# Norm sums gathered on four rows in the token mixers, and the first convolution tap on ScalarE

## The reference

```python
def rmsnorm(x, g):
    y = x32 * lax.rsqrt(jnp.mean(x32 * x32, axis=-1, keepdims=True) + EPS)
def l2norm(x):
    return x32 * lax.rsqrt(jnp.sum(x32 * x32, axis=-1, keepdims=True) + EPS)

# token_mixers: GLA, RetNet, gated DeltaNet (GDN), Mamba-2 (SSD)
oa = rmsnorm(oa, gla_norm) * silu(gg)          # 4 heads of 128 channels; ret the same
cqkv = silu(causal_conv(dqkv, state, w))       # 4 taps, 1024 channels
q = l2norm(heads(cq, 4)) * GDN_DK ** -0.5      # 4 heads of 64 channels
k = l2norm(heads(ck, 4))
oc = rmsnorm(oc, gdn_norm) * silu(dg)
xbc = silu(causal_conv(sxbc, state, w) + b)    # 4 taps, 768 channels
od = rmsnorm(yd, ssd_norm)                     # 2 groups of 256 channels
out = sum(sigmoid(mg) * (branch @ w_branch)) @ w_out
```

## Time and profile before

| | |
|---|---|
| runs without profile | 2736.95, 2736.98 and 2749.7 us, median 2736.98 |
| profiled execution | 2750.4 us, of which the span of the trace is 2748.3 |
| busy, share of the span | PE 90%, DVE 59%, ACT 39%, POOL 7% |
| mean granted TensorE clock | 0.914 |
| reciprocals in the mixers | 10 on DVE: eight of 128x1152, two of 128x576 |
| first taps on DVE | 28, 12.4 us in all |

### The profile page before, as it was taken

One profiled execution on the slowest core, in us unless ns is written; L12 is line 12 of the kernel. 1 busy time (PEld: TensorE's weight loads), 2 busy tenths in 40 slices (PEclk: granted clock), 3 DMA queues, 4 the chain that ended last, 5 costly groups with the idle time before them and its releaser, 6 DMA issues.

```text
span 2748.3 us, 38217 instructions
## 1 busy us (share of the span) xinstructions
PE 2462.7 (90%) x14436; PEld 2124.5 (77%) x14436; DVE 1628.5 (59%) x2112; ACT 1074.4 (39%) x1450; POOL 178.8 (7%) x247
## 2 busy tenths in 40 slices
PE   8899868868999989889778879899999999999996
PEld 7788758857699978779678766678878778787786
DVE  4453554264366463544553443387887878778785
ACT  3322321112033343324221121166766667567563
POOL 0210101111000000211011201000000000000000
PEclk8889879778899999999889688799999999999999
DMA  5224321021345432323311122288988889889871
GB/s 192 93 82 141 117 74 50 31 97 39 137 146 166 164 129 93 105 103 115 125 54 47 59 70 72 90 309 301 333 294 317 303 300 331 294 299 321 299 282 74
DMA packets 122566, 456.43 MB, mean 166 GB/s; under 512 B 14056, under 2 KB 14474, under 8 KB 120018
## 3 DMA queue, kind: packets, MB, share of 16 engines
q1 hardware_dynamic: 118818, 432.66, 44.6%
q0 software_dynamic: 3632, 22.12, 2.2%
HBM read 443.72 MB, written 11.00 MB: 165 GB/s over the span
## 4 chain that ended last, share of the span: by engine, by line
PE 77%; DVE 11%; issue 5%; ACT 4%; DMA 1%; POOL 1%; DVEq 0%; SPq 0%; ACTq 0%; POOLq 0%
PE ps L715 9%; PE ps L717 8%; PE ps L716 8%; PE ps L762 5%; DVE weights_low L2220 4%; PE ps L1265 4%; PE ps L1267 3%; PE ps L1266 3%; PE ps L1287 3%; PE ps L1288 3%; PE ps L1289 3%; PE ps L1238 3%; PE ps L756 2%; PE ps L896 2%; DMA ring<-in_stream 1%
## 5 line engine op out<-in xcount | busy, mean ns | idle before, releaser
L715 PE MATMUL ps<-u_high,tiles_high 128*128 128x288 f32 x1688 | 535.1, 317 | 2.6 <-DVE arena L1712 2.6
L716 PE MATMUL ps<-u_low,tiles_high 128*128 128x288 f32 x1688 | 521.3, 309 | 0.0
L717 PE MATMUL ps<-u_high,tiles_low 128*128 128x288 f32 x1688 | 519.1, 307 | 0.0
L1688 DVE TENSOR_TENSOR tiles_low<-ring,tiles_high 128x1024 fp32r<-128x1024 f32 x238 | 291.7, 1229 | 268.7 <-ACT tiles_high L1346 267.6
L715 PEld LDWEIGHTS ps<-u_high,tiles_high 128*128 128x128 f32 x1688 | 340.8, 202 | 12.7 <-issue 6.7
L1346 ACT ACTIVATE tiles_high<-ring 128x1024 fp32r<-128x1024 f32 x238 | 250.7, 1054 | 245.9 <-DMA ring<-in_stream 155.9
L716 PEld LDWEIGHTS ps<-u_low,tiles_high 128*128 128x128 f32 x1688 | 341.0, 202 | 0.6
L717 PEld LDWEIGHTS ps<-u_high,tiles_low 128*128 128x128 f32 x1688 | 340.3, 202 | 0.0
L2220 DVE TENSOR_TENSOR weights_low<-expert_ring,weights_high 128x1024 fp32r<-128x1024 f32 x288 | 334.3, 1217 | 4.9 <-ACT weights_high L1597 2.2
L1265 PE MATMUL ps<-weights_high,u_high 128*128 128x512 f32 (+1 forms) x768 | 297.6, 388 | 23.2 <-DVE weights_low L2220 22.6
L2220 DVE TENSOR_TENSOR weights_low<-ring,weights_high 128x1024 fp32r<-128x1024 f32 x240 | 280.1, 1217 | 42.9 <-ACT weights_high L1597 41.8
(11 more groups left out here) (381 smaller groups left out, 3377.6 us busy)
## 6 DMA issues: line engine op xcount, KB each, us to landing
ring<-in_stream SPq DMA_DIRECT2D x530, 512.0 KB, 4.2
expert_ring<-in_stream SPq DMA_DIRECT2D x288, 512.0 KB, 5.5
arena<-in_state POOLq DMA_DIRECT2D x8, 1024.0 KB, 5.2
state_s<-arena POOLq DMA_DIRECT2D x8, 1024.0 KB, 4.2
const<-in_const SPq DMA_DIRECT2D x1, 2052.5 KB, 12.0
arena<-in_const POOLq DMA_DIRECT2D x2, 832.0 KB, 4.9
h<-in_x SPq DMA_DIRECT2D x1, 1152.0 KB, 5.1
y<-acc POOLq DMA_DIRECT2D x1, 1152.0 KB, 4.4
```

What stands on the lines that cost most here:

```text
L715: mm(out, hi[k], uh[:, k, :], start=k == 0, stop=False)
L716: mm(out, hi[k], ul[:, k, :], start=False, stop=False)
L717: last = mm(out, lo[k], uh[:, k, :], start=False, stop=k == KD - 1)
L1688: tt(t_low[:, q % HELD, :], ring[:, (t % RING) * TILE:(t % RING + 1) * TILE], t_high[:, q % HELD, :].bitcast(F32), ALU.subtract).then_inc( ...
```

## The change

- Output norm, all four mixers. `out_sums` uses a constant `row_of` (7 columns, a one in the fourth) so that block `r` lands in row `r` of one bank: four matmuls as before, but accumulated to 4x288 (for SSD rows 0 and 1). Root and reciprocal take 4x288.
- PE then spreads the rows back: `spread_rows`, one matmul of four contraction rows to a block, 128x288 out (4 matmuls, for SSD 2), into the banks in which the sums were. DVE multiplies out of PSUM.
- Because the spread values lie in the banks that `states` writes, `states` now waits for the reciprocal (`row_ready`), spreads, and then waits for `o_final`, that is, for DVE's product.
- Keys and queries. The sums go to 32 rows of one bank through `row_pick`, root and reciprocal take 32x288, and PE spreads with eight matmuls of 32 contraction rows onto 64 partitions each, after its fill slot 7. The reciprocal stands after block 6 of the convolution on DVE, not after block 7.
- Convolution. The first tap moves from DVE (L1908) to ACT, as an Identity with scale and bias, into three `cbuf` buffers in place of two, two blocks ahead; from the fourth block on it waits for the block three before to be finished.

```diff
 def out_sums(L, n):
-    pe.wait_ge(osq_ready, m + 1)
-        for b in range(4):
-            last = mm(bank(M + b)[:, 0:TOK], C("ones"), tmp4[:, b, :], start=True, stop=True)
+    pe.wait_ge(osq_ready, 5 * L + ROWS_AT[n] + 1)
+    for b in range(4):
+        r = b // 2 if n == SSD else b
+        last = mm(bank(M)[0:4, 0:TOK], C("row_of", 3 - r, 7 - r), tmp4[:, b, :], start=b == 0, stop=b == 3)
+def spread_rows(L, n):
+    pe.wait_ge(row_ready, 5 * L + ROWS_AT[n] + 1)
+    for b in range(2 if n == SSD else 4):
+        last = mm(bank(M + b)[:, 0:TOK], C("ident")[0:4, b:b + 1].to_broadcast([4, P]), rs4[0:4, 0, :],
+                  start=True, stop=True)
+    last.then_inc(row_ps, 1)
 def states(L, n):
-    pe.wait_ge(ort_ready, m + 1)
+    spread_rows(L, n)
     pe.wait_ge(o_taken, L * NHEAD + HBASE[n] + HEADS[n])
+    pe.wait_ge(o_final, m + 1)
...
 # ACT, conv()
+    tap(0)
+    tap(1)
     for b in range(NCONV[n]):
+        if b + 2 < NCONV[n]:
+            tap(b + 2)      # b + 2 >= 3: waits conv_ready
         fill(L, n, b)
         act.wait_ge(convsum_ready, c + 1)
...
 # DVE, out_norm()
-    V.reciprocal(rs4[:, 0:w, :], rs4[:, 0:w, :]).then_inc(dve_step, 1)
+    V.reciprocal(rs4[0:4, 0, :], rs4[0:4, 0, :]).then_inc(row_ready, 1)
+    dve.wait_ge(row_ps, 5 * L + ROWS_AT[n] + 1)
-        last = tt(o4, g4, rs4, ALU.mult)
+        last = tt(o4, g4, ps_t[:, M:M + 4, 0:TOK], ALU.mult)
```

More of the change, by code:

```diff
@@ L170, in constants @@
     c["slot_col"] = np.arange(P)[:, None] * 1.0
+    c["row_of"] = np.tile(np.arange(7)[None, :] == 3, (P, 1)) * 1.0
     c["ret_decay"] = c.pop("ret_decay")
@@ L230 @@
 Q_OF = {t: q for q, t in enumerate(SPLIT)}
+ROWS_AT = [0, 1, 3, 4]
+QK_ROWS = 2
 NORM_AT = {0: 0, 1: 1, 2: 2, 3: 3, 5: 4}
@@ L1012, in gdn @@
                 pe.wait_ge(state_new, 4 * L + 2)
-                pe.wait_ge(qksq_ready, L + 1)
+                pe.wait_ge(osq_ready, 5 * L + QK_ROWS + 1)
                 for b in range(4):
-                    last = mm(bank(M + b)[:, 0:TOK], C("halfones"), tmp4[:, b, :], start=True, stop=True)
-                last.then_inc(qksum_ps, 1)
+                    last = mm(bank(M)[0:32, 0:TOK], C("row_pick", 15 - b, 47 - b), tmp4[:, b, :], start=b == 0, stop=b == 3)
+                last.then_inc(osum_ps, 1)
                 for s in range(5, 8):
                     fill(L, GDN, s)
+                pe.wait_ge(row_ready, 5 * L + QK_ROWS + 1)
+                for b in range(4):
+                    for i in range(2):
+                        last = mm(bank(M + b)[64 * i:64 * i + 64, 0:TOK],
+                                  C("ident")[0:32, 16 * i + b:16 * i + b + 1].to_broadcast([32, 64]), rs4[0:32, 0, :],
+                                  start=True, stop=True)
+                last.then_inc(row_ps, 1)
                 fill(L, GDN, 8)
@@ L1456, in out_norm @@
                 fill(L, n, slot)
[L1457 to L1462, removed]
+                act.wait_ge(osum_ps, 5 * L + ROWS_AT[n] + 1)
+                A(rs4[0:4, 0, :], bank(M)[0:4, 0:TOK], ACT.Sqrt, scale=1.0 / (256 if n == SSD else 128),
+                  bias=C("eps")[0:4]).then_inc(ort_ready, 1)
                 for s in range(slot + 1, NSLOT[n]):
@@ L1477, in conv, with tap @@
             def conv(L, n):
+                def tap(b):
+                    ci = CONV0[n] + b
+                    if b == 0:
+                        act.wait_ge(pads_ready, 2 * L + (1 if n == GDN else 2))
+                        act.wait_ge(o_taken, L * NHEAD + HBASE[n])
+                    if b >= 3:
+                        act.wait_ge(conv_ready, 14 * L + ci - 2)
+                    A(cbuf[:, b % 3, 0:312], zblk(n, b)[:, 0:312], ACT.Identity, scale=PVc("conv_w", ci),
+                      bias=PVc("conv_b", ci)).then_inc(tap_ready, 1)
+                tap(0)
+                tap(1)
                 for b in range(NCONV[n]):
                     c = 14 * L + CONV0[n] + b
+                    if b + 2 < NCONV[n]:
+                        tap(b + 2)
                     fill(L, n, b)
@@ L1906, in conv @@
                     src = zblk(n, b)
-                    out = cbuf[:, b % 2, 0:312]
-                    ts(out, src[:, 0:312], wv[:, 0, ci:ci + 1], PVc("conv_b", ci), ALU.mult, ALU.add).then_inc(dve_step, 1)
-                    dve.wait_ge(dve_step, steps.next())
+                    out = cbuf[:, b % 3, 0:312]
+                    dve.wait_ge(tap_ready, 14 * L + ci + 1)
                     stt(out, src[:, 1:313], wv[:, 1, ci:ci + 1], out, ALU.mult, ALU.add).then_inc(dve_step, 1)
@@ L1917, in conv @@
                         fill(L, n, b - 1)
+                    if n == GDN and b == nb - 1:
+                        dve.wait_ge(ort_ready, 5 * L + QK_ROWS + 1)
+                        V.reciprocal(rs4[0:32, 0, :], rs4[0:32, 0, :]).then_inc(row_ready, 1)
                 finish(nb - 1)
@@ L2024, in gdn @@
                 conv(L, GDN)
[L2025 to L2029, removed]
+                dve.wait_ge(row_ps, 5 * L + QK_ROWS + 1)
+                stt(cv[:, 0:2, :], cv[:, 0:2, :], 0.125, ps_t[:, M:M + 2, 0:TOK], ALU.mult, ALU.mult)
+                tt(cv[:, 2:4, :], cv[:, 2:4, :], ps_t[:, M + 2:M + 4, 0:TOK], ALU.mult).then_inc(qk_ready, 1)
                 dve.wait_ge(qk_ready, L + 1)
```

31 lines of the change are left out of this document (12 added, 19 removed).

## The result

The changed kernel takes 2765.6 us (median of five runs, 2764.5 to 2769.0); the kernel before, measured beside it, 2737.0 (2736.3 to 2749.7). The ratio is 1.0093 with an interval of 1.0071 to 1.0116: slower by 28.6 us. Forecast were 2760 us and 2741 to 2776.

The account below looks back on a forecast made before the run. PE, busy 90% of the span, was taken to bound the kernel. 27.6 - 2.2 + 13.7 - 2 x (7.35 + 0.8) = +22.8 us on the 2737.0 median gave 2760 us, range 2741 to 2776.

Parts of the forecast that it names:

- Reciprocals off the path, and short: Output norms: the reciprocals, 51.6 us of DVE, lie wholly beside PE's work; 288 columns take 1.95 us.
- Spread and wait on PE, +27.6: Eight output norms: spread, product wait and hand-overs fall on PE, 3.6 us in GLA, RET, GDN, 3.1 in SSD.
- RET relief, -2.2: RET norms: DVE's product is over before `states`, so POOL's masks are quicker by 1.1 us, twice.
- The clock, +13.7: `states` behind each output norm: first L954 block at 3.67 us in place of 1.96, 1.7 a norm, eight norms.
- its upper bound: Clock in `states`: at most all 11 blocks that run at full clock today are slowed, 18.8 us.
- Keys, -7.35 a layer: Key/query norms: the reciprocal moves into DVE's idle time and the spread is covered, gaining 7.35 us a layer.
- late next: Key/query norms: once the reciprocal has moved, the last convolution block's finish on DVE is the next thing late.
- Tap, -0.8 a layer: Convolution: of the taps moved to ACT, only two before the last L1712 count, 0.8 us a layer.
- The sum: Whole kernel: all terms together make +22.8 us, slower, 2760 us.
- The clock doesn't care: Rival: the spread keeps PE busy and first `states` blocks stay at full clock; +4 to +9, 2741 to 2746; chance 0.20.
- Taps in the way: Rival: waiting taps on in-order ACT hold tanh and weight copies; at most +12.6, 2772; chance 0.15.
- Absorbed: Rival: later `states` meets shorter PE waits if transfers or ACT's copies set the pace; -16.3 stays, 2721; chance 0.05.

Follow-up runs that it names:

- twice: The changed kernel with each output-norm spread issued twice, nothing else: 2783.0 us (1.0161), 17.4 over the changed kernel.
- the fastest version: The change without its output-norm part, with the last tanh and the key/query products moved ahead of tile work: 2713.7 us (0.9917).
- experiment 6: Change without output norm, last tanh and key/query products ahead of tile work: 2713.7 us; also with 128-row key spread, 2715.9, or tap back on DVE, 2719.4.
- norm_only: The output-norm part of the change alone, key/query norm and convolution as in the kernel before: 2800.9 us (1.0216).
- late_wait: The changed kernel with PE's wait for the output product moved behind the first eight matmuls of `states`: 2770.0 us (1.0113).
- experiment 1: Parts of the change, each beside the kernel before: output norm alone 2800.9 us, keys alone 2728.4, tap alone 2741.6, all but the output norm 2721.9.

## Why the prediction was right, point by point

- **Reciprocals off the path, and short:** right. 1.94 us on 4 rows (1.95 taken), no PE wait for it in any of the eight norms, and the 36 us that DVE saves on them bring nothing.
- **Spread and wait on PE, +27.6:** right. 2.20 + 1.54 against 2.10 + 1.46, and 1.23 + 1.97 against 3.1 in SSD, 28.8 in all; `twice` shows that the spread counts. The 0.1 us for two hand-overs was an assumption; the wait of 1.54 beside DVE's product of 1.35 makes it 0.2.
- **RET relief, -2.2:** right. POOL's pair, against the earlier trace rows, is not stretched any more. PE's wait for it fell from 2.69 to 1.11 us in RET and from 1.57 to 1.11 in GLA, 1.1 more, as forecast. RET costs 1.1 and 2.8 us less than GLA by place; 1.7 of the 2.8 is GLA's second block in layer 1, which had run at 2.4 GHz before:

```profile
308.47 2.04 POOL L2416 TENSOR_TENSOR arena<-arena,const 32x512 f32<-32x512 f32 x2 [18.66 <-PE ps L962]
```

  One reading of the prediction is wrong here, without an effect on the sum: it had the two stretched each other "by less than a whole instruction". The single instructions before say otherwise. POOL's first mask takes its usual 1.03 us (303.39 to 304.42); DVE's product, from 303.84, ends at 305.64, 1.22 behind it; POOL's second, from 304.39, takes 2.15 and ends at 306.54, 0.90 behind the product. The 3.15 us from the first to the last are nearly the sum of what the three take alone (1.03, 1.36, 1.03), so they ran one behind the other and not side by side.

- **The clock, +13.7:** right in kind, short in size. I let the clock fall where it had fallen before, as the first L954 block begins, and charged one block a norm. It fell in the new idle time, ahead of `states` (0.95 in the stretch of the spread, 0.50 behind it), and took all 11 blocks that had been at 2.4 GHz, 18.8, which the prediction had as its upper bound. SSD is part of it: one block a norm charged, two lost. The bound was too low as well: 18 groups of 128-row matmuls in `states` went from 0.66 to 1.13 us or a little less, 8 us that stood in no term, and shorter waits for POOL (1.57 to 1.11 in GLA and GDN; in an SSD 1.85 to 0.39, three waits together) took 5.7 back. So the clock cost 21 by place. Wide matmuls give back 18 to 20 of it by place (6 and 13 by the medians), so the term is measured and not only argued. The norms by place come to 47.8 where the prediction's terms are 39.1.
- **Keys, -7.35 a layer:** right, -7.8. The spread was at the lower of the two values (2.15 us for both halves), so it was hidden with 3.7 us to spare; PE's wait behind it is 4.35 and not "about 2", because the finish, late by the tanh, sets the end whatever the spread takes. What the prediction said would be late next was so.
- **Tap, -0.8 a layer:** right by place, 0.95 a layer, in the wait that was named. The first `br` tiles wait as before, and the taps' idle-time cover held, though DVE's new waits for them came as a surprise. The medians don't show it: the tap alone is +4.3, in the fastest version it is worth 5.7, and most of either is in no row that I can name.
- **The sum:** +22.8 forecast, +28.6 measured. The norms were 8.7 short, 7.5 of it the clock; keys and taps gained 1.2 more than forecast; and in the two traces 4.8 came back in stretches that the change doesn't touch. That last part nobody had forecast, so the total is nearer than its terms deserve, and that is luck. The two traces from the first norm on differ by 25.6, 3 less than the medians.
- **Rivals.** "The clock doesn't care": false, 0 of 20 blocks at 2.4 GHz. "Taps in the way" as the cause of 12 us: false by place. "Absorbed": false; the first `br` wait is 7.09 as before and every norm's delay stays.

## What to carry to other kernels

Before making an operation shorter on one engine, look whether anyone waits for it: here 50 us of reciprocals were free, and the two that were waited for only had to be issued earlier. A trip through PE between two steps of another engine puts that engine's step on PE's path. If its matmuls use few rows, it can also cost PE its clock for what comes after: here in all eight output norms, where it stood ahead of further narrow matmuls, but in only one of four places at the keys with 1.59 us idle behind it (experiment 6). Try the wide form, which costs no more columns. Where a kernel runs with its clock moving between two levels, measure edits of under 20 us by place as well as by the median, and expect the two to differ, here by up to 18 us.

## What was unexpected on the hardware

- Two spreads of nearly equal length (2.20 and 2.10 us) and with 1.54 us idle behind both, from 4 rows and from 128, left the granted clock at 0.50 and at 1.00.
- Unchanged, gapless matmuls take 19.2 or 25.4 us, at 1.00 or 0.73, in kernels whose edits lie hundreds of microseconds ahead of them (`norm_only`, `late_wait`). That the edits set the level there is not shown: the kernel before, too, had 122 tile matmuls at 0.68 in its profiled execution, and its 25 runs beside experiment 1 lie between 2733.6 and 2753.4.
- The tap as an ACT instruction with a scale and a bias per partition takes 0.65 us for 312 columns (below; min/median/max in ns), against 0.44 on DVE and 0.45 for the tanh of the same block on ACT.

```profile
L1498 ACT ACTIVATE arena<-arena,pv x28: 636/648/652, 333.0 to 1596.6; 128x312 f32<-128x312 f32 x28
```
